# A streaming encoder step: from the attention scores to the feed-forward by feature instead of by token

## The reference, cut to what matters

```
softmax_with_sink(s, sink):
    m = max(max(s), sink);  e = exp(s - m)
    return e / (sum(e) + exp(sink - m))
residual_tail(h, oa, ob):
    mixed = concat(rmsnorm(oa, g_out_a), rmsnorm(ob, g_out_b))   # 512 features each
    h = h + mixed @ w_out
    u = rmsnorm(h, g_ffn)
    return h + (silu(u @ w_gate) * (u @ w_up)) @ w_down          # hidden 2816
y = rmsnorm(h, g_final)
```

## Time and profile before

| | |
|---|---|
| median of 3 runs | 1499.74 us (1499.39 to 1500.48) |
| the profiled execution | 1497.76 us, its span 1496.0 us |
| TensorE | 1410.3 us busy (94%), granted clock 0.976 on average |
| VectorE | 579.4 us (39%) |
| ScalarE | 477.5 us (32%) |
| GpSimd | 214.1 us (14%) |
| transfers | 87.34 MB, 58 GB/s on average |

### The profile page before, as it was taken

How to read it: one execution, slowest core, us unless ns; L and a number is a source line. 1 busy time by engine, 2 the same in 40 slices (tenths; PEclk the granted TensorE clock), 3 DMA queues, 4 the chain that set the end, 5 groups by cost and what they waited for, 6 DMA issues and landing times.

```text
span 1496.0 us, 22497 instructions
## 1 busy us (share of the span) xinstructions
PE 1410.3 (94%) x9041; PEld 1303.2 (87%) x9041; DVE 579.4 (39%) x1374; ACT 477.5 (32%) x1044; POOL 214.1 (14%) x317
## 2 busy tenths in 40 slices
PE   5989987999999887999999999999999999999996
PEld 3878876877888756887999999999999999999996
DVE  6235542323232334444325242433333342425155
ACT  6336552354545473433321212021211112111103
POOL 2125542253524250000000000000000000000000
PEclk9999999999999898999999999999999999999998
DMA  7621113111212043112221111111111202020002
GB/s 193 111 60 30 34 44 98 44 47 41 90 41 73 23 135 124 43 40 64 85 79 38 54 43 43 43 43 43 43 43 42 61 25 71 15 73 30 12 1 116
DMA packets 104687, 87.34 MB, mean 58 GB/s; under 512 B 14336, under 2 KB 95328, under 8 KB 104072
## 3 DMA queue, kind: packets, MB, share of 16 engines
q1 hardware_dynamic: 104584, 85.91, 19.9%
HBM read 71.10 MB, written 14.89 MB: 57 GB/s over the span
## 4 chain that ended last, share of the span: by engine, by line
PE 87%; DVE 4%; ACT 3%; issue 3%; DMA 2%; POOL 1%; SPq 0%; DVEq 0%; ACTq 0%
PE ps L526 27%; PE ps L527 25%; PE ps L528 25%; PE ps L719 2%; PE ps L846 2%; DVE ps L1476 1%; PE ps L685 1%; DMA out<-outb 1%; PE ps L647 1%; DMA out<-raw 1%; PE ps L731 1%; PE ps L605 1%; ACT sp_x L1130 1%; ACT ph_x L1129 1%; DVE sp_w L1488 1%
## 5 line engine op out<-in xcount | busy, mean ns | idle before, releaser
L1682 DVE TENSOR_TENSOR outs<-outs,ps 128x384 f32<-128x384 f32 (+1 forms) x264 | 134.6, 510 | 108.7 <-PE ps L528 108.7
L1667 DVE TENSOR_TENSOR gu<-ps,sg 128x384 f32<-128x384 f32 (+1 forms) x66 | 34.6, 525 | 238.1 <-PE ps L528 238.1
L1834 POOL TENSOR_TENSOR pl_x<-sp_x,ph_x 128x512 fp32r<-128x512 f32 (+5 forms) x120 | 102.2, 866 | 149.4 <-ACT sp_x L1130 147.8
L1295 ACT ACTIVATE h_hi<-gu 128x384 fp32r<-128x384 f32 (+1 forms) x66 | 32.9, 498 | 222.7 <-DVE gu L1667 222.7
L1129 ACT ACTIVATE ph_x<-ps,negc 128x512 fp32r<-128x512 f32 (+5 forms) x120 | 63.1, 526 | 83.9 <-PE ps L731 83.9
L526 PE MATMUL ps<-f_hi,ff0hi 128*128 128x384 f32 (+1 forms) x264 | 85.7, 325 | 0.0
L526 PE MATMUL ps<-f_hi,ff3hi 128*128 128x384 f32 (+1 forms) x264 | 85.6, 324 | 0.0
L526 PE MATMUL ps<-f_hi,ff1hi 128*128 128x384 f32 (+1 forms) x264 | 85.6, 324 | 0.0
L526 PE MATMUL ps<-f_hi,ff2hi 128*128 128x384 f32 (+1 forms) x264 | 85.6, 324 | 0.0
L1289 ACT ACTIVATE sg<-ps 128x384 f32<-128x384 f32 (+1 forms) x66 | 30.5, 465 | 171.7 <-PE ps L528 171.7
L527 PE MATMUL ps<-f_lo,ff0hi 128*128 128x384 f32 (+1 forms) x264 | 85.2, 323 | 0.0
(11 more groups left out here) (290 smaller groups left out, 3799.5 us busy)
## 6 DMA issues: line engine op xcount, KB each, us to landing
raw<-in_w_gate SPq DMA_DIRECT2D x22, 512.0 KB, 5.2
raw<-in_w_up SPq DMA_DIRECT2D x22, 512.0 KB, 5.0
raw<-in_w_down SPq DMA_DIRECT2D x22, 512.0 KB, 4.0
raw<-in_w_in SPq DMA_DIRECT2D x14, 512.0 KB, 3.9
cb<-c_scratch SPq DMA_DIRECT2D x4, 1312.0 KB, 6.6
xt<-in_x_prompt SPq DMA_DIRECT2D x8, 512.0 KB, 4.3
out<-outb SPq DMA_DIRECT2D x16, 256.0 KB, 2.4
raw<-in_w_out SPq DMA_DIRECT2D x8, 512.0 KB, 3.5
```

The lines of the kernel that those rows point to most:

```text
L1295: act.activation(h_hi[par][:, f, c0:c0 + n], gu[(f + c) % 2][:, 0:n], ACT.Copy).then_inc(S["g_hi"], 1)
L1667: dve.tensor_tensor(gu[(f + c) % 2][:, 0:n], bank(3 + c, n), sg[c][:, 0:n], ALU.mult)\
L1682: add = dve.tensor_tensor(y, y, bank(6 + o % 2, whole * P).rearrange("p (t m) -> p t m", t=whole), ALU.add)
L1834: pool.tensor_tensor(pl_x[at][0:rows, 0:n], sp_x[at][0:rows, 0:n], ph_x[at][0:rows, 0:n].bitcast(F32), ALU.subtract).then_inc(S["x_pl"], 1)
```

## The change

Nothing is turned between the scores and the feed-forward but x itself.

- **Quotients by feature.** The products with values give, for each head, 64 rows of output and 64 equal rows of the sum. ScalarE copies the output rows of the two heads to one tile, and the sums' rows across partitions to another (in fox VectorE copies the sums). VectorE takes a reciprocal of the whole [128, columns] tile and multiplies.
- **Sinks.** exp(sink - m) is made earlier, split in two halves by GpSimd, turned together with the minima (the `amw` task), and added to the sums by one more product of a 0/1 matrix (`sinkw`).
- **Storage.** `o_scratch` is by feature; it is read back in three chunks of tokens (`oc`).
- **x.** In the last pair 18 tasks (`xt`, units 47 to 55) turn x tile by tile; VectorE copies, and SyncE stores it by feature in DRAM, from where `y_res` is loaded by chunk. The number of turns is 72.
- **Norms.** Squares of each 128-feature block (ScalarE) are added by GpSimd, and one f32 product with a matrix of 1/512 gives the mean in every row. ScalarE takes the square root of the matrix, VectorE the reciprocal and the scaling. Squares, sums and mean of the first chunk are placed in units 53 to 57, the rest in 58 to 60.
- **Output projection.** Now weights are the stationary side and a chunk's tokens the moving side: 3 chunks x 8 output blocks x 8 x 3 products, with the residual's squares and norm one chunk behind, and those of the next chunk in between.
- **Feed-forward.** `y_res` is [feature, token], so each addition is one instruction. The first group's order of products is changed so that the last chunk of tokens comes late.
- The stores of the window stage are issued at a step's end; one step and one unit less in each loop; g_out and g_ffn are loaded as columns instead of being spread over partitions.

```diff
 def window_values(u):                                             # TensorE
-    mm = product(out, vh, vl, xh, xl, w == WB0[u], w == WB0[u + 1] - 1)
-mm.then_inc(S["w_pv"], 1)
+    product(out, vh, vl, xh, xl, w == WB0[u], False)
+pe.matmul(out, sinkw[kv][:], am_w[u % 3][:, 0:2 * m], start=False, stop=True).then_inc(S["w_pv"], 1)
...
+for c, (_, n) in enumerate(CHUNKS):                               # TensorE, the output stage
+    for o in range(KB):
+        at = KB * c + o
...
+        if at >= 4:
+            pe.wait_ge(S["d_y"], at - 3)
+        for k in range(KB):
+            if o == 0:
+                pe.wait_ge(S["c_lo"], KB * c + k + 1)
+            mm = product(bank(OUT_BANKS[at % 4], n), wo_hi[:, o, k, :], wo_lo[:, o, k, :],
+                         mix[c][:, k, 0:n], mix_lo[c][:, k, 0:n], k == 0, k == KB - 1)
+        mm.then_inc(S["c_op"], 1)
+        if c >= 1 and o == 0:
...
+            residual_mean(c - 1, 4)
+        if c < 2 and o == 3:
...
+            group_means(c + 1)
...
+def window_quotient(u):                                           # VectorE, step u + 2
+    n = 2 * rows_of(WU[u][1])
+    o, den = ot_w[u % 2][:, 0:n], sx_w[u % 2][:, 0:n]
+    dve.wait_ge(S["w_ot"], 2 * u + 2)
+    dve.reciprocal(den, den).then_inc(S["w_den"], 1)
+    dve.wait_ge(S["w_den"], 2 * u + 1)
+    dve.tensor_tensor(o, o, den, ALU.mult).then_inc(S["w_den"], 1)
+
+def fox_quotient(v):                                              # VectorE, unit v + 1
...
+    for h in range(2):
+        own, other = slice(h * HD, (h + 1) * HD), slice((1 - h) * HD, (2 - h) * HD)
+        dve.wait_ge(S["x_pv"], 2 * v + h + 1)
+        dve.tensor_copy(sx_x[own, 0:n], ps[other, 6 + h, 0:n]).then_inc(S["x_sx"], 1)
+    dve.wait_ge(S["x_sx"], 2 * at + 2)
+    dve.reciprocal(sx_x[:, 0:n], sx_x[:, 0:n]).then_inc(S["x_den"], 1)
...
+    dve.tensor_tensor(og_x[:, 0:n], ot_x[:, 0:n], sx_x[:, 0:n], ALU.mult).then_inc(S["x_den"], 1)
...
+for c in range(3):                                                # ScalarE, the output stage
+    for o in range(KB):
+        if c >= 1 and o == 0:
+            residual_root(c - 1)
+        residual_square(c, o)
+        if c >= 1 and 1 <= o <= 3:
+            normed_hi(c - 1, range(3 * o - 3, min(3 * o, KB)))
+        if c < 2 and o <= 2:
+            group_squares(c + 1, range(3 * o, min(3 * o + 3, KB)))
+        if c < 2 and o == 3:
+            group_roots(c + 1)
+        if c < 2 and o >= 6:
+            mixed_hi(c + 1, range(4 * (o - 6), 4 * (o - 5)))
...
+for c in range(3):                                                # VectorE, the output stage
+    for o in range(KB):
+        residual_add(c, o)
+        if c >= 1 and o == 0:
+            residual_inverse(c - 1)
+        if c >= 1 and 1 <= o <= 3:
+            normed(c - 1, range(3 * o - 3, min(3 * o, KB)))
+        if c < 2 and o == 4:
+            group_inverses(c + 1)
+        if c < 2 and o in (5, 6):
+            mixed(c + 1, range(4 * (o - 5), 4 * (o - 4)))
...
+for c in range(3):                                                # GpSimd, the output stage
+    for o in range(KB):
+        if c < 2 and o <= 2:
+            group_sums(c + 1, range(3 * o, min(3 * o + 3, KB)))
+        residual_sums(c, o)
+        if c < 2 and o >= 6:
+            mixed_lo(c + 1, range(4 * (o - 6), 4 * (o - 5)))
...
 def add_down(q, last_weights=False):
-    y = y_res[:, 3 * c:3 * c + whole, o, :]
-    add = dve.tensor_tensor(y, y, bank(6 + o % 2, whole * P).rearrange("p (t m) -> p t m", t=whole), ALU.add)
-    if n % P:
-        y = y_res[:, 3 * c + whole, o, 0:n % P]
-        add = dve.tensor_tensor(y, y, ps[:, 6 + o % 2, whole * P:n], ALU.add)
+    y = y_res[:, o, c0:c0 + n]
+    dve.tensor_tensor(y, y, bank(6 + o % 2, n), ALU.add).then_inc(S["d_y"], 1)
```

More of the change, by code:

```diff
@@ L26 @@
 FFQ = FF // (2 * P)
-Y_SET = 4 * 9
+Y_SET = 8 * 3
 CHUNKS = ((0, 384), (384, 384), (768, 288))
@@ L197, in make_schedule @@
     keyed = 1
-    for s in range(NWU + 2):
+    for s in range(NWU + 1):
         if s + 2 < NWU:
@@ L231, in make_schedule @@
             task(("x", v, 3), "amx", i, 2)
+        if v - XT0 in range(TILES):
+            for half in range(2):
+                task(("x", v, 3), "xt", v - XT0, half)
         if j == 3 and 0 <= v < NX:
@@ L300, with out_loads, gate_up_done, squares_used @@
     RAW_IN.append(W_SLOT0[_n % 3])
+def out_loads(k):
+    return 1 if k < PAIRS else 2
 def raw_in_out(k):
-    return W_SLOT0[k % 3] + k // 3 + 1
+    return W_SLOT0[k % 3] + sum(out_loads(n) for n in range(k % 3, k + 1, 3))
+OUT_BANKS = (2, 3, 6, 7)
+FIRST_GATE_UP = ((0, 0), (0, 1), (1, 0), (1, 1), (0, 2), (1, 2))
+def gate_up_done(q, f, w, c):
+    if q == 0 and f == 0:
+        return FIRST_GATE_UP.index((w, c)) + 1
+    return 12 * q + 6 * f + 3 * w + c + 1
+def squares_used(k):
+    return 3 * (k // 4) + max(1, k % 4)
 RAW_FFN = tuple(raw_in_out(k) for k in (6, 7, 5))
@@ L817, in _, with group_means @@
                 items("w", s, 3)
-                if 1 <= s <= NWU:
+                if s >= 1:
                     window_values(s - 1)
                 items("w", s, 4)
-            for v in range(-LEAD, NX + 2):
+            def group_means(c):
+                n = CHUNKS[c][1]
+                for g in range(2):
+                    pe.wait_ge(S["c_acc"], 6 * c + 3 * (g + 1))
+                    pe.matmul(bank(4 + g, n), onesm[:], root[g][:, 0:n], start=True, stop=True).then_inc(S["c_ss"], 1)
+            for v in range(-LEAD, NX + 1):
                 items("x", v, 0)
@@ new lines, in gate_up @@
+                        for k in range(KB):
+                            if q == 0 and f == 0 and (w, c) == (0, 2):
+                                pe.wait_ge(S["c_fl"], 2 * KB + k + 1)
+                            mm = product(bank(3 * w + c, n), ff[x][0][:, k, :], ff[x][1][:, k, :],
+                                         f_hi[:, k, c0:c0 + n], f_lo[:, k, c0:c0 + n], k == 0, k == KB - 1)
+                        mm.then_inc(S["g_mm"], 1)
+                        if q == 0 and f == 0 and (w, c) == (0, 0):
+                            residual_mean(2, 7)
@@ L1029, in task @@
                     return
+                if kind == "amw" and a[0] == 0:
+                    window_sinks(0)
                 act.wait_ge(S["g_pe"], n + 1)
@@ L1182, in _ @@
             items("pre", 3)
-            window_sinks(0)
-            for s in range(NWU + 2):
+            window_sinks(1)
+            for s in range(NWU + 1):
                 items("w", s, 0)
@@ L1460, in task @@
+                    if tile == 0:
+                        dve.wait_ge(S["pr_pe"], 3 * NW)
+                    else:
+                        dve.wait_ge(S[f"xt_st{half}"], 16 * tile)
+                    dve.tensor_copy(xt_out[half][:, :, 0:m], bank(b, 4 * m).rearrange("p (k m) -> p k m", k=4))\
                        .then_inc(S["ev_dve"], 1)
```

755 lines of the change are left out of this document (400 added, 355 removed).

## The result

The changed kernel takes 1531.49 us (median of 4 runs, 1529.08 to 1531.87), the kernel before, beside it, 1500.11 (4 runs). The ratio is 1.0206, interval 1.0191 to 1.0221: **31 us slower**. Forecast were 1482.7 us and a range up to 1498. The profiled execution has a span of 1529.3 us, 33.3 more than before.

What follows compares the result with a forecast made beforehand. TensorE, busy 94% of the 1496.0 us span, was taken as the bound. Parts 1 and 2 minus 9, then - 5 - 4 + 3 - 2, made minus 17: 1480.8 profiled, 1482.7 median; forecast 1474 to 1491, range 1470 to 1498.

Steps and rivals of the forecast that it cites:

- Part 3, windows: Window stage: turns (7.8 us) and quotient waits (2.6) leave, sinks products (4.1) come in; minus 5 (minus 7 to plus 8).
- Rival (d): VectorE: reciprocals as cheap as additions, VectorE 6.6 us earlier, GpSimd then paces; 1479 us; chance 0.04.
- (a): Windows and fox: VectorE's in-order queue becomes the bound; 1498 us, no change; chance 0.16.
- Part 6, feed-forward: Feed-forward: the last chunk's addition as one instruction frees TensorE's bank sooner; minus 2 us.
- Part 4, pairs 0 to 2: Fox pairs 0 to 2: 7.5 us of turns and waits leave, 4 given back; minus 4 (minus 8 to plus 6).
- at unit 12 the minima of unit 13 are queued behind it: Fox pairs 0 to 2: minima wait behind the 512-column quotient on VectorE, TensorE for their bank; 1 to 2 us a pair.
- Part 5, last pair to unit 53: Last pair up to unit 53: turns and quotient waits leave, x turns and transfers come in; plus 3 (minus 4 to plus 12).
- it just fits; I add 3 us: Last pair: about 8.6 MB of transfers in some 25 us, 344 GB/s against 374, fit; 3 us added.
- Rival (b): Last pair: x's detour through DRAM makes copies wait for stores to land; slower, 1508 or 1525 us; chance 0.13.
- Part 2, way in: From unit 53's scores to the output stage: work moved ahead costs 5.6 us more than the wait replaced (0 to 9).
- eight scalings of 0.57: Way in: VectorE's eight scalings behind the reciprocals, 4.6 us in all.
- Part 1, output stage: Output stage: 121.0 us removed, 106.5 added (products 93, ones products 7, joints 6.5); gain 14.5 (11 to 23).

Runs made afterwards that it cites:

- e4: Changed kernel with two orders altered: next chunk's norm squares ahead of the first residual square, first window's sinks earlier; 1512.54 us, ratio 1.0088.
- f1: e4 with the division of 512-column fox chunks, except the last but one, in two pieces, one and two units after the copies; 1493.93 us, ratio 0.9963.
- f2: f1 with x's first tiles loaded earlier, four buffers instead of two for x turned, pair 0's decays loaded first; 1489.52 us, ratio 0.9928.
- f3: f2 with the first chunk's 1.5 MB load split, its windows half loaded early, x turns one unit earlier, squares respread; 1490.23 us, ratio 0.9925.
- e2: Changed kernel with the reciprocal of each fox quotient taken over 32 columns only; 1510.97 us, ratio 1.0072.
- c1: Changed kernel with 15 idle TensorE products in place of the wait behind unit 14's scores; 1527.11 us in a single run.
- e1: Changed kernel without the 18 tasks turning x, their loads and stores; the residual is loaded straight from x_prompt, unturned; 1514.04 us, ratio 1.0099.
- g1_early_turns: f1 with pair 0's decays loaded first and x turned, copied and stored at the kernel's start instead of in the last pair; 1490.60 us, ratio 0.9939.
- e3: Kernel before the change with two idle 240-column reciprocals on VectorE at each of 8 places of a 512-column fox quotient; 1505.61 us, ratio 1.0051.
- g2_band_early: g1_early_turns with the bias band written behind the load of x's tile 5, two window cache copies behind the weights; 1512.99 us, ratio 1.0093.

## Why the prediction was wrong

The sum was minus 17, the profile says plus 33.3. By its own steps:

- **Part 3, windows: minus 5, measured -6.5.** Right in mechanism and size. In the kernels whose first window is not held up (e4, f1, f2, f3) it is -3.9 to -4.4, so some 2 us of the 6.5 only offset the late start. VectorE was busy 84.4 of 110.5 us, forecast 86 of 117; the reciprocal of 256 columns took 1.742 us, forecast 1.75, of 512 columns 3.353, forecast 3.33. Rival (d) is out, and so is (a) for the windows.
- **Part 6, feed-forward: minus 2, measured -0.9.** The ledger's -2.0 has in it the 1.1 us of the last tile's turns, which the sum had under part 1. Small, and mis-sized by 1.1.
- **Part 4, pairs 0 to 2: minus 4, measured +9.3.** The step "at unit 12 the minima of unit 13 are queued behind it ... 1 to 2 us a pair" named the right wait and priced it as a wait. It was 3.4, 1.9 and 2.0 us, and the clock behind it was left out: the three boundaries cost 13.5 us. e2, c1 and f1 show both. The other term, 7.5 us of turns and waits removed, was right: f1, in which the quotient holds nothing up, gains 7.8. This is rival (a) in fox, at the three boundaries and again in the last pair (e2), and at none of the 18 window steps.
- **Part 5, last pair to unit 53: plus 3, measured +14.3.** The step "it just fits; I add 3 us" compared bytes with a peak rate. The bytes were right, 8.80 MB from unit 47 to 53, but they took 40 us and not 25, at a share of 0.75. What it cost was a single tile that came late (4.4 us of waiting), turns held by other tasks (3.7 and 2.7), and a clock of 0.72. Units 47 to 55 took 6.6 us each, over the 5 that the prediction names as a sign of being wrong, but not with stores that landed late. Rival (b) had the detour as the cause and the landing of the stores as the way. These landed in 3.6 us (median). VectorE did wait 12.4 us for them, but f2, where that wait is gone, still waits as long for the loads. e1 prices the detour at 17 us in these units, and e2 the quotient of unit 48, for which the step had a wait of some 2.5 us, at 8.4; the two overlap.
- **Part 2, way in: plus 5.6, measured +10.8.** The first group of products ended 45.0 us after the scores of unit 53 began (574.05 to 619.10), forecast 39.7. Two steps failed. VectorE's two copies began 23.1 us after these scores and not 19.4: TensorE had waited 3.3 us for a tile of x, which the sum has nowhere. And "eight scalings of 0.57" took 8.0 us, not 4.6 (last section).
- **Part 1, output stage: minus 14.5, measured -2.9**: 118.1 us from where the first group would have started at full pace (614.9), against 121.0. The terms themselves were nearly right: e4_order, counted the same way, takes 105.0 us where 106.5 were forecast, with joints of 4.2 and 3.7 us (3.8 and 2.7 forecast) and some 3 us of ones products (7 forecast; 0.5 each). What failed is a step that is not there: the sum never asks when the squares in the middle of a chunk are ready. They stood behind a 1.5 MB load.
- **Not in the sum at all: the start, +5.3, and windows to unit 0, +4.1.** The first window's turn now waits 3.6 us for the sinks, which ScalarE makes behind a table load of 1.28 us; with the sinks earlier the start is 105.0 to 107.6 and not 109.6 to 112.0, which is most of it. In the second place TensorE waited 2.3 us for the first minima; the decays' load behind others in the queue made up 3.3 us (f2).

The terms that are right are the durations; those that are wrong are the queues. Of the 50 us between forecast and result 17 lie in parts 1 and 2, 13 in part 4, 11 in part 5, 1 in part 6 and 9 where I did not look, less 1.5 of part 3. With five orders changed and two buffers more, at the same work, the kernel is 0.7% faster than the one before (f2_deeper, 1489.52, 0.9928), still 7 us short of the forecast. The last pair and the way in still take 80.2 us in it, against 67.8 before and 68.5 in g1_early_turns. So what is left there is the detour.

## What to carry to other kernels

For every instruction that is moved into an in-order queue, ask what is next behind it and which engine waits for that; split it, or put it behind, before judging the change. A wait of TensorE in a full stretch costs more than its length: 7.5 us for 3.4 in the changed kernel, 6.0 for 1.6 in e3. So look at the granted clock of the stretch behind it. Where a change adds traffic to a stretch, the fit of the bytes says little; look for the tiles that stand behind a large transfer in the queue, and expect the wait to move, as in f3, when only that transfer is moved.

## What was not expected of the hardware

VectorE slows down beside GpSimd when both its operands are in SBUF. The same subtraction of 384 columns took 0.61 us each where GpSimd was idle, and 1.31 where it added. An addition of 384 columns with one operand in PSUM (L1693) took 0.55 to 0.56 either way. VectorE in the changed kernel, in order of time (the sum of the two instructions of a row):

```profile
673.82 1.23 DVE L1707 TENSOR_TENSOR f_lo<-f_raw,f_hi 128x384 fp32r<-128x384 f32 x2
...
683.73 2.62 DVE L1707 TENSOR_TENSOR f_lo<-f_raw,f_hi 128x384 fp32r<-128x384 f32 x2
```

and GpSimd beside it, idle between 670.92 and 674.87 and adding at 683.36:

```profile
670.12 0.80 POOL L1971 TENSOR_TENSOR root_a<-root_a,sqo 128x288 f32<-128x288 f32 x1 [0.56 <-ACT sqo L1244]
674.87 0.84 POOL L1971 TENSOR_TENSOR root_a<-root_a,sqo 128x288 f32<-128x288 f32 x1 [3.95 <-ACT sqo L1244]
...
683.36 2.58 POOL L1992 TENSOR_TENSOR sums_h<-sums_h,sqh 128x384 f32<-128x384 f32 x2
```

GpSimd pays too: 1.29 us a sum (sums_h) there, 0.99 alone. The Trainium skill ("GPSIMD Engine Reference", 1. Specifications) says that GpSimd's way to SBUF is shared with VectorE, with contention where a VectorE instruction has two SBUF inputs; the trace agrees. It fits the eight scalings of the way in too: the first three, before or as GpSimd begins, took 0.52 to 0.61 us each, the five beside its lower halves 1.35 to 1.37. VectorE's two rows, then GpSimd's:

```profile
607.42 2.85 DVE L1668 SCALAR_TENSOR_TENSOR oc<-oc,small,root_a 128x384 f32<-128x384 f32 x4
610.18 5.23 DVE L1668 SCALAR_TENSOR_TENSOR oc<-oc,small,root_b 128x384 f32<-128x384 f32 x4
608.57 9.63 POOL L1977 TENSOR_TENSOR ol<-oc,mix 128x384 fp32r<-128x384 f32 x8 [4.80 <-ACT mix L1258]
```

A broadcast write of 1.5 MB from 8 partitions took about 35 us (f1_pieces: issued at 24.7, its readers issued at 59.9). Two copies of 48 KB issued right behind it in the same queue took 15.8 and 25.3 us to land; in g2_band_early, where they are issued later, 3.3 and 2.7.
